# A two-layer streaming trunk: the mLSTM mixer's heads rewritten, four samples at a time and the prompt as one causal product

## What is computed

```python
def step(carry, inp):                       # one chunk, one head
    C, n, m = carry
    qb, kb, vb, ib, fb = inp
    b = jnp.cumsum(fb, axis=-1)
    lw = jnp.where(causal, b[..., :, None] - b[..., None, :] + ib[..., None, :], -jnp.inf)
    lp = b + m[..., None]
    mj = jnp.maximum(lp, jnp.max(lw, axis=-1))
    w, wp = jnp.exp(lw - mj[..., None]), jnp.exp(lp - mj)
    s = jnp.einsum('bhjd,bhsd->bhjs', qb, kb) * w
    num = jnp.einsum('bhjs,bhsv->bhjv', s, vb) + wp[..., None] * jnp.einsum('bhvd,bhjd->bhjv', C, qb)
    den = jnp.sum(s, axis=-1) + wp * jnp.einsum('bhd,bhjd->bhj', n, qb)
    h = num / jnp.maximum(jnp.abs(den), jnp.exp(-mj))[..., None]
    ...                                      # C_new, n_new: decayed old state plus sum of v k^T, k
hC = _head_layernorm(hC, p['mlstm_norm'][c]).reshape(B, T, C_INNER) + p['mlstm_skip'][c] * xc
x = x + (hC * jax.nn.silu(zg)) @ p['w_down1'][c]
```

## Time and profile before

| | us |
|---|---|
| median of 3 runs | 2386.26 (2384.49 to 2390.1) |
| profiled execution, its own time | 2387.82 |
| its span, first to last instruction | 2386.0 |
| mean granted TensorE clock | 0.968 of full speed |
| the second mixer's heads, with their tail | 1206 to 1773 |

### The profile page before, as it was taken

One profiled execution on the slowest core, in us unless ns is written; L12 is line 12 of the kernel. 1 busy time (PEld: TensorE's weight loads), 2 busy tenths in 40 slices (PEclk: granted clock), 3 DMA queues, 4 the chain that ended last, 5 costly groups with the idle time before them and its releaser, 6 DMA issues.

```text
span 2386.0 us, 35273 instructions
## 1 busy us (share of the span) xinstructions
PE 2233.5 (94%) x13637; PEld 1985.8 (83%) x13637; DVE 1008.2 (42%) x1342; ACT 474.7 (20%) x695; POOL 845.1 (35%) x492
## 2 busy tenths in 40 slices
PE   6999997899999999999999898998979899999997
PEld 5898996899999998999875564745559899999996
DVE  4565565432220025793236566474642322220025
ACT  4333333211110002221221302213110211100011
POOL 4323321545454545554401000010115454444443
PEclk9999999899999999999999899998989999999998
DMA  4121221212222222322223416062352122222222
GB/s 165 52 89 54 84 87 38 71 62 70 77 73 78 72 77 90 117 79 100 94 87 145 176 48 251 22 229 93 139 198 71 62 71 76 73 75 75 77 73 88
DMA packets 57295, 224.24 MB, mean 94 GB/s; under 512 B 6288, under 2 KB 11280, under 8 KB 48272
## 3 DMA queue, kind: packets, MB, share of 16 engines
q1 hardware_dynamic: 48576, 202.94, 24.1%
q10 hardware_dynamic: 8656, 20.39, 2.3%
HBM read 170.06 MB, written 53.25 MB: 94 GB/s over the span
## 4 chain that ended last, share of the span: by engine, by line
PE 78%; DVE 10%; issue 4%; DMA 3%; ACT 3%; DVEq 1%; POOL 0%; SPq 0%; ACTq 0%; POOLq 0%
PE psd L204 10%; PE psd L208 9%; PE psd L209 9%; PE psd L205 9%; PE psd L211 9%; PE psd L210 9%; PE psm L1217 3%; DMA Cs<-st_c 3%; DVE cv L902 2%; PE psd L1126 2%; PE psm L1188 2%; DVE ntmp L277 2%; PE psm L1224 2%; PE psd L1224 2%; PE psm L382 2%
## 5 line engine op out<-in xcount | busy, mean ns | idle before, releaser
L1722 POOL CAST whi<-wraw 128x1024 fp32r<-128x1024 f32 x224 | 238.7, 1066 | 963.9 <-PE psd L211 504.8
L1724 POOL TENSOR_TENSOR wlo<-wraw,whi 128x1024 fp32r<-128x1024 f32 x224 | 543.4, 2426 | 17.9
L204 PE MATMUL psd<-xh,whi 128*128 128x320 f32 x1280 | 407.3, 318 | 31.7 <-ACT xh L250 19.1
L208 PE MATMUL psd<-xl,whi 128*128 128x320 f32 x1280 | 402.4, 314 | 10.8 <-POOL xl L285 8.7
L205 PE MATMUL psd<-xh,whi 128*128 128x320 f32 x1280 | 399.2, 312 | 0.0
L209 PE MATMUL psd<-xl,whi 128*128 128x320 f32 x1280 | 398.7, 312 | 0.0
L210 PE MATMUL psd<-xh,wlo 128*128 128x320 f32 x1280 | 398.7, 311 | 0.0
L211 PE MATMUL psd<-xh,wlo 128*128 128x320 f32 x1280 | 398.5, 311 | 0.0
L204 PEld LDWEIGHTS psd<-xh,whi 128*128 128x128 f32 x1280 | 243.9, 191 | 35.9 <-issue 29.5
L208 PEld LDWEIGHTS psd<-xl,whi 128*128 128x128 f32 x1280 | 243.1, 190 | 18.9 <-POOL xl L285 13.8
L205 PEld LDWEIGHTS psd<-xh,whi 128*128 128x128 f32 x1280 | 244.0, 191 | 0.8 <-issue 0.2
(11 more groups left out here) (355 smaller groups left out, 3377.1 us busy)
## 6 DMA issues: line engine op xcount, KB each, us to landing
wraw<-w SPq DMA_DIRECT2D x224, 512.0 KB, 3.2
Cs<-st_c SPq DMA_DIRECT2D x32, 1024.0 KB, 6.7
c_s<-Cs SPq DMA_DIRECT2D x32, 1024.0 KB, 4.7
z_kept<-zb ACTq DMA_DIRECT2D x16, 320.0 KB, 2.2
ztp<-z_kept SPq DMA_DIRECT2D x4, 1024.0 KB, 5.4
c_p<-Cp SPq DMA_DIRECT2D x4, 1024.0 KB, 3.9
xT<-x SPq DMA_DIRECT2D x4, 640.0 KB, 6.7
x_kept<-xT ACTq DMA_DIRECT2D x1, 2560.0 KB, 8.6
```

Of the source, the lines that this page charges most:

```text
L204: pe.matmul(o0, wh, x0, start=st, stop=False)
L208: pe.matmul(o0, wh, l0, start=False, stop=False)
L1722: pool.tensor_copy(whi[s][:], wraw[s][:]).then_inc(w_high, 1)
L1724: pool.tensor_tensor(wlo[s][:], wraw[s][:], whi[s][:].bitcast(F32), ALU.subtract).then_inc(w_split, 1)
```

## The change

It rewrites the heads of `MLstm` and their queues:

- Samples go in two sets (even, odd), four at a time: a unit is one quarter of the state's rows (128 of 512) for the four samples of a set, again 1 MB in one of three buffers, in runs of 2 KB where there were 8 KB. The read is four products with 32 stationary columns each, to partitions 32j; the update four products over 32 rows each, to four banks.
- The prompt is one causal product over all 512 tokens: off-diagonal score blocks, scaled by decays, then numerators from all blocks at once. The state is summed over the four blocks by products between the units, and ACT copies it out.
- The division by the denominator is gone: its square, scaled by epsilon, is added to the sums of squares, and the layer norm's root takes both.
- A head's sample tail lies beside the next head's projections. The gate's product, the low parts and the block weights go from DVE to GpSimd; the three rows lie at partitions 0, 32 and 64; the heads are written out with no hardware loop.
- In all norms and in mixer 0, the activation table that holds both Ln and Exp is loaded ahead (`ln_exp_set`).

```diff
+        def ln_exp_set(a):
+            a.preload_act_table_set("natural_log_exp_and_others")
...
             def act(self, a):
+                ln_exp_set(a)
...
-        Cs = [sb(f"Cs{s}", [P, KH, DH], at=x3) for s in range(2)]
+        Cs = [sb(f"Cs{s}", [P, NB // 2, DH], at=x3) for s in range(2)]
...
+            def pe_read(self, pe, h, u):
+                par_, k = self.unit(u)
+                s, n = divmod(NB * h + u, 3)[::-1]
+                pe.wait_ge(self.cin[s], 16 * (n + 1))
+                for j in range(KH):
+                    mm = pe.matmul(B[1][32 * j:32 * (j + 1), :], qz[:, par_, k, 32 * j:32 * (j + 1)], Cs[s][:, j, :],
+                                   start=False, stop=(u == NB - 1), skip_group_check=True)
...
+            def pe_update(self, pe, h, u):
+                par_, k = self.unit(u)
+                for j in range(KH):
+                    pe.wait_ge(*((V_.sem, V_.at(("C", u - 1, j), h)) if u else (S_.sem, S_.at(("num", j), h))))
+                    pe.matmul(U[j], ktok[32 * j:32 * (j + 1), NP, tt(k)], vm[par_][32 * j:32 * (j + 1), :], start=True,
+                              stop=True).then_inc(P_.sem, 1)
...
+                pick = [con[0:H, CON["sel"] + P * h:CON["sel"] + P * (h + 1)], sel3[32:32 + H, tt(h)], sel3[64:64 + H, tt(h)]]
+                three = list(zip(pick, (rowM, rowW, rowE), (pD[1], pM[1], pM[0])))
+                for w, row, o in three:
+                    pe.matmul(o[:, 0:SEQ], w, row[:, 0:SEQ], start=True, stop=True)
...
+                for k in range(KH):
+                    pe.wait_ge(V_.sem, V_.at(("qh", k), h))
+                    for c in range(NP - 1):
+                        mm = pe.matmul(off[c], kT[:, k, tt(c)], qT[:, k, P * (c + 1):SEQ], start=(k == 0 and c < 2),
+                                       stop=(k == KH - 1), skip_group_check=True)
...
+                for f in range(KH):
+                    for c in range(NP):
+                        pe.matmul(U[f][:, tt(c)], vtok[:, c, tt(f)], att[:, tt(c)], start=(c == 0), stop=(c == 0),
+                                  skip_group_check=True)
+                pe.matmul(B[0], ones, att[:, 0:SEQ], start=True, stop=False, skip_group_check=True)
+                pe.matmul(B[1], att[:, tt(NP)], vtok[:, NP, :], start=True, stop=False, skip_group_check=True)
+                pe.wait_ge(S_.sem, S_.at(("off", NOFF - 1), h))
+                part = [att[:, off_at(c):off_at(c + 1)] for c in range(NP - 1)]
+                for f in range(KH):
+                    for c in range(NP - 1):
+                        mm = pe.matmul(U[f][:, P * (c + 1):SEQ], vtok[:, c, tt(f)], part[c], start=False,
+                                       stop=(c == NP - 2), skip_group_check=True)
...
+                for u in range(NB):
+                    self.pe_read(pe, h, u)
+                    if u == 0:
+                        pe.wait_ge(V_.sem, V_.at("vm1", h))
+                    self.pe_update(pe, h, u)
+                    if u == 2:
+                        ...
+                        pe.matmul(B[0], ones, kT[:, 0, 0:SEQ], start=True, stop=True).then_inc(P_.sem, 1)
+                    if u == 6:
+                        ...
+                        pe.matmul(B[0], ones, kT[:, 0, 0:SEQ], start=True, stop=True).then_inc(P_.sem, 1)
+                        ...
+                        pe.matmul(bank[0][:, 0:P], ones, att[:, tt(NP)], start=True, stop=False)
+                        for k in range(KH):
+                            pe.matmul(bank[0][:, 0:P], ones, rt[:, k, :], start=False, stop=(k == KH - 1))
+                        for k in range(KH):
+                            for c in range(NP):
+                                pe.matmul(bank[0][:, P + k:P + k + 1], ktok[:, c, tt(k)], ones[:, 0:1], start=(c == 0),
+                                          stop=(c == NP - 1))
+                            mm = pe.matmul(bank[0][:, 2 * P + NB * k:2 * P + NB * (k + 1)], ktok[:, NP, tt(k)],
+                                           con[:, CON["ind"]:CON["ind"] + NB], start=True, stop=True)
+                    k = u // 2
+                    ...
+                    for c in (0, 1) if u % 2 == 0 else (2, 3):
+                        mm = pe.matmul(bank[k % 2], ktok[:, c, tt(k)], vtok[:, c, :], start=(c == 0), stop=(c == NP - 1))
...
+                for u in range(NB):
+                    self.vec_beside(v, h, u)
+                    o, k = self.unit(u)
+                    for j in range(KH):
+                        v.wait_ge(P_.sem, P_.at(("su", u, j), h))
+                        C, b = Cs[(NB * h + u) % 3][:, j, :], NP + 2 * j + o
+                        v.scalar_tensor_tensor(C, C, dec[:, b:b + 1], U[j], ALU.mult, ALU.add).then_inc(V_.sem, 1)
...
             def pool_head(self, pool, h):
...
+                self.blocks(pool, h, 2)
+                if h:
+                    self.pool_z(pool, h - 1, range(2))
+                self.blocks(pool, h, 3)
+                if h:
+                    self.pool_z(pool, h - 1, range(2, KH))
+                    self.pool_lo(pool, h - 1)
...
+                def load(n):
+                    s, i = n % 3, n // 3
+                    if i:
+                        sp.wait_ge(self.cst[s], 16 * i)
+                    sp.dma_start(Cs[s][:], part(io["st_c"], n // NB, n % NB)).then_inc(self.cin[s], 16)
...
+                for h in range(H):
+                    for u in range(NB):
+                        n = NB * h + u
+                        store(n)
+                        if u == 2:
+                            if h:
+                                sp.wait_ge(self.GT.sem, self.GT.at("zS", h - 1))
+                            for z, c0, c1 in ((ztp, 0, SEQ), (zts, SEQ, T)):
+                                sp.dma_start(z[:], io["z_kept"][KH * h:KH * (h + 1), :, c0:c1].rearrange("k p c -> p k c"))\
+                                    .then_inc(self.zin, 16)
+                        if n >= 1 and n + 2 < NB * H:
+                            load(n + 2)
...
-            pool.wait_ge(mlstm.V.sem, mlstm.V.at(("z", KH - 1), H - 1))
+            mlstm.pool_z(pool, H - 1, range(KH))
+            pool.wait_ge(mlstm.GT.sem, mlstm.GT.at(("z", KH - 1), H - 1))
             split(U_DN1, 0, U_DN1 // 2, True)
-            pool.wait_ge(mlstm.V.sem, mlstm.V.rounds(H))
+            mlstm.pool_lo(pool, H - 1)
+            mlstm.pool_sample(pool, H - 1)
+            pool.wait_ge(mlstm.GT.sem, mlstm.GT.rounds(H))
             split(U_DN1 + 1, 1, U_DN1 // 2, True)
```

More of the change, by code:

```diff
@@ L793, in trunk @@
         pM = [flat(psm[:, 2 * s:2 * s + 2, :]) for s in range(2)]
-        U = [psd[0][:, 0, :], psd[0][:, 1, :], bank[2], bank[3]]
+        B = [psd[0][:, 0, :], psd[0][:, 1, :], psd[1][:, 0, :], psd[1][:, 1, :]]
+        U = [B[2], B[3], bank[2], bank[3]]
+        off_at = lambda c: T + P * sum(NP - 1 - i for i in range(c))
         tiles5 = range(NP + 1)
@@ L801, in trunk @@
         Z_FIRST = 10
[L803 to L806, removed]
         class MLstm:
@@ L1060, in vec @@
                     v.wait_ge(self.zst[s], 16 * CI // 2)
-                with v.Fori(0, H - 1) as h:
-                    self.vec_head(v, h, True)
-                self.vec_head(v, H - 1, False)
+                v.memset(qz[:], 0.0).then_inc(self.qz0, 1)
+                for h in range(H):
+                    self.vec_head(v, h)
+                self.vec_tail(v, H - 1)
             def pe(self, pe):
@@ new lines, in pe_tokens @@
+            def pe_tokens(self, pe, h, k, between=None):
+                P_, V_, S_ = self.P, self.V, self.S
+                ft, w = KH * h + k, blk[k % 2]
+                if k:
+                    pe.wait_ge(V_.sem, V_.at(("x", k - 1), h))
+                for t in range(NP):
+                    pe.matmul(B[2][:, tt(t)], xp[:, ft, NCONV - 1 + P * t:NCONV - 1 + P * (t + 1)], w[:, 2, :],
+                              start=True, stop=True)
+                if k == 0:
+                    pe.wait_ge(self.X, h + 1)
+                pe.matmul(bank[3][:, tt(1)], xs[:, k, :], w[:, 2, :], start=True, stop=True)\
+                    .then_inc(P_.sem, 1)
+                if between is not None:
+                    between()
+                pe.wait_ge(S_.sem, S_.at(("x", k), h))
+                if k:
+                    pe.wait_ge(S_.sem, S_.at(("tk", k - 1), h))
+                for t in range(NP):
+                    pe.transpose(B[3][:, tt(t)], kT[:, k, tt(t)], ident)
+                pe.transpose(bank[3][:, tt(0)], kT[:, k, tt(NP)], ident).then_inc(P_.sem, 1)
@@ L1483, in act_head @@
-                for t in range(2, NP):
-                    num(t)
-                a.activation(att1[:, 0:SEQ], pD[1][:, 0:SEQ], ACT.Abs).then_inc(S_.sem, 1)
-                for b in range(2, 5):
-                    queries(b)
+                a.wait_ge(V_.sem, V_.at(("ex", NP), h))
+                a.activation(att[:, 0:T], att[:, 0:T], ACT.Exp).then_inc(S_.sem, 1)
```

(17 more changed lines are left out.)

846 lines of the change are left out of this document (393 added, 453 removed).

## The result

| | before | after |
|---|---|---|
| median, us | 2386.22 | 2268.06 |
| lowest to highest | 2384.49 to 2390.1 | 2260.29 to 2275.56 |
| profiled execution | 2387.82 | 2260.29 |

What follows compares the result with a forecast made beforehand. Matmuls were taken to bound the kernel (TensorE busy 94%), with small steps in the tail; 2387.8 - 133.9 + 2.3 - 6.4 - 1.5 = 2248.3 us for the profiled execution, 2247 as median, range 2198 to 2300.

Steps and rivals of the forecast that it cites:

- TensorE's removed work: Heads of the second mixer: a causal product replaces the prompt's 37 us recurrence; a head takes 104.9 us, before 137.
- Row groups: Sample state update: four products in row groups run at once, 1.1 us an update instead of 3.43.
- Rival (a): Sample updates: row groups do not overlap, an update stays at 3.43 us, 2291 us in all; chance 0.16.
- Who ends last in a unit: Sample part: state loads pace the units, each step 0.4 us issue + L + 5.0; unit 7 ends at 56 us.
- L: Time of a state's load beside a store in the sample part: 7 to 8 us, bounds 4.5 and 8.4.
- Projection part: Head's projections and tokens with the previous head's tail: 17.8 us, the tail's DVE, ACT and GpSimd steps lying beside.
- GpSimd: Work moved to GpSimd, some 19 us a head more: cost bound 0 to 4 us a head, taken as 0.
- Last tail: Exposed stretch from last addition to next dense product: 21.1 us, before 18.8, so +2.3.
- Tables: Second activation table load gone: -6.4 us in five norms, -1.5 us in mixer 0.
- (b): Sample part: transfers are quicker, L = 5.5 us, 9 us a head less, 2211 us; chance 0.18.
- (c): Sample part: clock stays at the lower level through most of it, +11 us a head, 2291 us; chance 0.09.
- (d): States' 2 KB runs halve the transfer rate or worse, slower than before; 2421 us at L = 22; chance 0.02.

Runs made afterwards that it cites:

- ACT's order alone: Changed kernel with the previous head's sample square and scale on ACT moved behind the query copies of tiles 2 and 3; 2261.5 us.
- sums_early: Changed kernel with the samples' denominator and n sums (25 small products) moved on TensorE from behind update 6 to behind update 3; 2250.5 us.
- all_with_vector: Changed kernel with third state and gate values loaded ahead, small sums behind update 3, samples' ACT steps behind query copies, gate product on DVE; 2238.9 us.
- states_first: Changed kernel with third state and gate values loaded ahead, ACT's square and TensorE's variance product later, unit 6's state products ahead of the small sums; 2230.3 us.

## Why the prediction was right, and where 12 us came from

**TensorE's removed work: right.** The prompt takes 23.4 us from scores to last product, against 6.8 + 17.8 = 24.6. Head 1 takes 109.2 us (first projection to the next head's) against 104.9.

**Row groups: right.** 1.07 us an update against 1.1. Rival (a), 0.16, is out: the four start together. The Trainium skill ("TensorE: Matmul & The Clock Gate", Measured speedup vs the span model) gives 3.07x for this form; the trace has 3.43 / 1.07 = 3.2.

**Who ends last in a unit: right, each step a little short.** From the first read, ends of units forecast and measured in head 1:

| unit | 0 | 1 | 2 | 3 | 4 | 5 | 6 | 7 |
|---|---|---|---|---|---|---|---|---|
| forecast | 5.0 | 8.9 | 17.4 | 23.2 | 33.8 | 37 | 46.7 | 56 |
| measured | 4.9 | 8.9 | 19.7 | 24.7 | 38.0 | 43.0 | 50.8 | 62.9 |

The step that failed is the constant 5.0 us for "read, update and additions". Behind a wait the read and the update run at the lower clock, 2 us each for 1.0 and 1.1, so units 2 and 4 take 6.6 and 6.7 us from landing to end: 3.3 us. L was near: 7.8 us at unit 2 and 7.4 at unit 6, median 8.1 over 32 loads, for "7 to 8 us". I had set 3 us a head aside for the clock elsewhere; it belonged in this chain, where it is paid in series with the load. Unit 7 is a second one: 12.1 us after unit 6 for my 9.3, of which 1.9 us are the state products in front of it (3.55 us for 1.7) and most of the rest is the variance and the small products (6.6 us, from 1391.52 to 1398.09, for 5.9). Together the part takes 62.9 for 56; from it go my separate 3 for the clock and 2 for changes of the array's split, of which nothing more can be read.

**Projection part: the term that was wrong.** "Its DVE, ACT and GpSimd steps lie beside the projections": 22.5 us from the first projection to the scores, for 17.8. Not their length but their place in ACT's queue costs TensorE 3.0 us, and 1.6 more at a lower clock behind that (busy 19.4 for 17.8). ACT's order alone took 2.6 to 3.0 us off; with TensorE's variance product later as well the part loses no more than the wait for GpSimd's blocks.

**GpSimd: right in kind.** The bound was 0 to 4 us a head, and I took 0. The skip, a DVE step with two SBUF inputs, took 4.75 us beside GpSimd's product and 2.73 without, and the additions of the states, with one PSUM input, kept 736 to 749 ns in the whole trace, as I had read from the earlier trace rows. The Trainium skill ("SBUF — State Buffer", Who interferes with whom) says that a DVE step with at most one input from SBUF, outside its two-port modes, does not contend with GpSimd, and one with two inputs does. The rows agree: 2.0 us more for the skip's four steps. In the last tail four 128-column steps with two inputs took 5.47 us beside GpSimd's low parts, where one takes 0.35 elsewhere in the same trace. But its price in the sum is what ACT's queue made of it, and the run that removed it showed no gain.

**Next projection:** 0.4 us after the last addition, for 1.5. **Last tail:** 23.1 us for 21.1, had 18.8. The slow DVE steps are half of the 2 us: L1433's four take 5.47 us, and GpSimd waits 1.0 us for the step behind them; most of the rest is GpSimd's four gate products, 6.20 us beside DVE's skip for the 5.1 of the sum. **Tables:** 7.9 us in the run of its own for 6.4 + 1.5; the interval leaves 5 to 11.

**The balance.** From the first head's projection to the last addition 424.4 us were measured (1200.3 to 1624.7) for 414.1: +10.3. The tail adds 2.0. 2248.3 + 12.3 = 2260.6, and the execution took 2260.29. The rest of the span fits as well: outside heads and last tail it is 1811.0 us for 1819.2 before, 8.2 less for the tables' forecast 7.9. The 10.3 is a balance of errors of both signs, so the closeness is in part luck. In head 1 the projection part is 4.7 us over and the sample part 6.9, while the separate 5 for clock and array split, 1.2 of the prompt's part and 1.1 of the next projection's wait were not needed. And head 0 took 97.3 us where the terms give 104.9 - 2.5 - 3 + 1.5 = 100.9, so the other three are 13.9 over. The 8 us from the profiled execution to the median are, as far as the two profiled executions show, the spread at unit 7: this was the fastest execution, and the one with the lower clock at unit 6 has 13 us more in its sample parts.

**Rivals.** (b), shorter loads, is out: 8.1 us median, and 6.6 even with a quarter of the stores. (c), the clock, is there for about half of its 11 us a head: the 3.3 at units 2 and 4 and the 1.9 ahead of unit 7, with 0.86 granted over the part. (d) is there at 0.4 us a load, not 14.5; by its own terms before would have been reached at 35 us a head (139 / 4), not 37.

**Open:** why the clock behind unit 6's wait differs between executions of the same kernel. No run here changed it on purpose.

## What to carry to other kernels

Where loads pace a chain, price each link with the clock that the engine has behind the wait, not with the one it has in a busy stretch. And when work moves beside other work, draw each engine's queue in its new order: three places (ACT's square, SP's third load and gate values, TensorE's variance product) held 39 us that order alone gave back. A fix that fills a wait and one that removes the same wait don't add up.

## What the chip showed that I had not expected

A run of products with one and eight columns lets the granted clock fall although TensorE is shown busy without a hole. The changed kernel around unit 6's small sums, which begin at 1392.5 (columns as in the earlier trace rows; the clock is third from last):

```profile
1393.00:1395.00 2.00, 2.00 (x21) 2.00 (x20) 1.33 (x3) 1.00 (x2) 0.00 (x0) 1.00 0.62 225
1395.00:1397.00 2.00, 2.00 (x20) 2.00 (x20) 0.00 (x0) 0.00 (x0) 0.00 (x0) 1.00 0.88 324
1397.00:1399.00 2.00, 2.00 (x12) 1.57 (x12) 0.26 (x2) 0.28 (x1) 0.00 (x0) 0.72 0.97 255
1399.00:1401.00 2.00, 2.00 (x4) 0.67 (x2) 0.00 (x0) 0.00 (x0) 0.00 (x0) 0.50 1.05 409
```

The lower level, 1.2 GHz, then meets products that had run at twice the rate. In the two kernels that moved the sums (sums_early, all_with_vector), the state products right behind them are slow at the new place, 3.27 and 3.76 us in head 1, and where the state products went ahead of the sums (states_first) they are not. What in such a run lets the clock fall is not shown. And a product with one column costs as much as one with 128: four of them (eight passes) took 0.95 to 1.03 us, 0.24 to 0.26 each, against 0.237 in the earlier trace rows. PEld, the weight load, is busy for 2.00 of 2 us in the first two rows: each product loads 128 columns of weights, whatever it multiplies.
